# Five orders changed on ScalarE, VectorE and GpSimd in a transformer kernel of three-part products

## What the reference computes

```python
# first block
h = rms_norm(x, g) * (1 + sc1) + sh1
glu_in, qk_in, v, o_pre, if_pre, merge_pre = split(h @ w_in + b_in)
a = glu_in[..., :C] * sigmoid(glu_in[..., C:])
a = silu(layer_norm(causal_depthwise_conv(a, conv_dw_w, conv_dw_b)))   # 31 taps
y_conv = a @ w_conv_pw + b_conv_pw
hm = mlstm_chunkwise(q, k, v, i_pre, f_pre)                            # 4 heads
hm = (hm - mean(hm)) * rsqrt(var(hm) + EPS) * mlstm_norm_g             # per head
y = (g_conv * y_conv + g_mlstm * sigmoid(o_pre) * hm) @ w_out          # g_*: sigmoid(merge_pre)
# second block: mixer A with FFN, then mixer B with FFN
mem_n = rmsnorm(mem, g_mem)                                            # 256 memory rows
q, k, v, q_mem = split(rmsnorm(x, g_mix) @ b_w_in)                     # mixer B
q, k = apply_partial_rope(q), apply_partial_rope(k)
o = banded_window_attention(q, k, v)                                   # 16 heads, 4 key heads
x = x + concat(o, memory_cross_attention(q_mem, mem_n, w_mem_kv)) @ b_w_out
```

## Time and profile before

| | |
|---|---|
| Time, median of 3 runs | 2068.83 us |
| The profiled execution | 2069.17 us |
| Its span in the profile | 2067.4 us |
| TensorE busy | 2034.8 us (98 %) |
| VectorE busy | 1198.1 us (58 %) |
| ScalarE busy | 938.9 us (45 %) |
| GpSimd busy | 1018.3 us (49 %) |
| Granted clock of TensorE, mean | 0.998 |

### The profile page before, as it was taken

The page is one execution under the profiler, slowest core; times in us unless marked ns, Lnnn a source line. Parts: engine busy times, 40 slices in busy tenths (PEclk is TensorE's granted clock), DMA queues, the critical chain, the costliest instruction groups (busy, mean ns, idle before and its releaser), DMA issues.

```text
span 2067.4 us, 30134 instructions
## 1 busy us (share of the span) xinstructions
PE 2034.8 (98%) x11590; PEld 1743.2 (84%) x11590; DVE 1198.1 (58%) x2215; ACT 938.9 (45%) x1525; POOL 1018.3 (49%) x483
## 2 busy tenths in 40 slices
PE   9999999999999999999999999999999999999998
PEld 6888977788898989876877888989887588889997
DVE  4889788673642434476985463646423935545563
ACT  3345545363432334534366552434432956434343
POOL 3433432434675666443713575657344036665663
PEclk9999999999999999999999999999999999999999
DMA  9654322235233333332211433333433024333422
GB/s 370 241 183 143 103 62 62 87 103 175 70 102 102 107 98 103 96 110 66 80 24 52 127 102 97 98 113 93 147 92 74 2 85 114 103 102 102 122 73 92
DMA packets 282550, 220.91 MB, mean 107 GB/s; under 512 B 13520, under 2 KB 266576, under 8 KB 280112
## 3 DMA queue, kind: packets, MB, share of 16 engines
q1 hardware_dynamic: 271712, 195.75, 31.2%
q10 hardware_dynamic: 10704, 23.33, 3.7%
HBM read 213.56 MB, written 2.10 MB: 104 GB/s over the span
## 4 chain that ended last, share of the span: by engine, by line
PE 82%; DVE 8%; ACT 3%; POOL 3%; issue 2%; DMA 1%; ACTq 0%; SPq 0%; DVEq 0%; POOLq 0%
PE bank L1046 57%; PE bank L1123 11%; PE bank L1343 2%; PE bank L1534 2%; PE bank L1556 2%; DVE arena L3219 1%; PE bank L1491 1%; DVE small L3217 1%; PE bank L1543 1%; PE bank L1644 1%; POOL entry L3296 1%; PE bank L1391 1%; POOL w_split L3263 1%; DVE bank L2565 1%; PE bank L1402 1%
## 5 line engine op out<-in xcount | busy, mean ns | idle before, releaser
L1046 PE MATMUL bank<-h_hi,w_split 128*128 128x512 f32 x2832 | 865.3, 382 | 2.3 <-DVE arena L3087 1.1
L3263 POOL TENSOR_TENSOR w_split<-wslots,w_split 128x2048 fp32r<-128x2048 f32 (+3 forms) x119 | 470.1, 3951 | 648.2 <-ACT w_split L1798 636.6
L1046 PEld LDWEIGHTS bank<-h_hi,w_split 128*128 128x128 f32 x2832 | 534.7, 189 | 93.5 <-issue 16.2
L1046 PE MATMUL bank<-h_lo,w_split 128*128 128x512 f32 x1416 | 537.5, 380 | 0.0
L1798 ACT ACTIVATE w_split<-wslots 128x2048 fp32r<-128x2048 f32 (+2 forms) x114 | 194.1, 1702 | 367.9 <-PE bank L1046 314.9
L1046 PE MATMUL bank<-hid_hi,w_split 128*128 128x512 f32 x1056 | 316.5, 379 | 1.3 <-POOL w_split L3305 0.9
L1046 PEld LDWEIGHTS bank<-h_lo,w_split 128*128 128x128 f32 x1416 | 267.8, 189 | 38.7 <-issue 3.4
L1046 PEld LDWEIGHTS bank<-hid_hi,w_split 128*128 128x128 f32 x1056 | 199.6, 189 | 31.1 <-issue 1.6
L1046 PE MATMUL bank<-hid_lo,w_split 128*128 128x512 f32 x528 | 200.1, 379 | 0.0
L3296 POOL TENSOR_TENSOR entry<-entry_sum,entry 128x512 fp32r<-128x512 f32 x108 | 155.8, 1467 | 80.0 <-ACT entry L2121 80.0
L2565 DVE SCALAR_TENSOR_TENSOR bank<-arena,cols,bank 128x512 f32<-128x512 f32 x240 | 161.3, 750 | 5.4 <-ACT bank L1912 4.9
(11 more groups left out here) (376 smaller groups left out, 3142.5 us busy)
## 6 DMA issues: line engine op xcount, KB each, us to landing
wslots<-in_f_w_up SPq DMA_DIRECT2D x88, 512.0 KB, 5.0
wslots<-in_w_in SPq DMA_DIRECT2D x24, 1024.0 KB, 5.4
wslots<-in_w_ffn_up SPq DMA_DIRECT2D x44, 512.0 KB, 4.7
arena<-in_w_ada ACTq DMA_DIRECT2D x8, 2048.0 KB, 10.2
wslots<-in_a_w_in SPq DMA_DIRECT2D x10, 1024.0 KB, 5.3
arena<-in_w_ada_first SPq DMA_DIRECT2D x8, 1024.0 KB, 18.9
wslots<-in_f_w_down SPq DMA_DIRECT2D x8, 1024.0 KB, 5.1
wslots<-in_f_w_down SPq DMA_DIRECT2D x16, 512.0 KB, 4.0
```

Source lines behind the costliest of these rows:

```text
L1046: return nc.tensor.matmul(bank[:], w, woven(x), start=start, stop=stop)
L3263: last = nc.gpsimd.tensor_tensor(part[:, 1, cols_of], slot(p, 1, size)[:, 0, cols_of], part[:, 0, cols_of].bitcast(F32), ALU.subtract)
```

## The change

Five orders change; nothing is added to or left out of the computation.

- On VectorE, the last head's reciprocal goes ahead of the head's last four taps.
- On ScalarE, the split for the first conv_pw job (the one that `conv_gates(2)` began with) goes from behind the eighth upper of the convolution to behind the fifth.
- On ScalarE, the squares of the memory go ahead of the uppers of conv_pw job 0.
- On ScalarE, in the late stage of b_mix, the split that stood ahead of tile 6's upper goes behind that tile's square and copy.
- For mixer B's keys, ScalarE issues the four copies ahead of the value copies, both still behind the value product, and GpSimd rotates the keys ahead of the lower part of b_qmem.

```diff
@@ -2064,8 +2064,9 @@
                     last.then_inc(bank_free[one("merge_conv", 0)[0]], 1)
                 nc.scalar.activation(xT[:, c, :], conv(c), ACT.Square).then_inc(S["ln_square"], 1)
 
-            def conv_gates(j):
-                p = started("merge_conv", j)
+            def conv_gates(j, p=None):
+                if p is None:
+                    p = started("merge_conv", j)
                 for m in range(2):
                     last = nc.scalar.activation(halves(conv_gate[:, 2 * j + m, :]), plain(banks[2 * p + m][:]), ACT.Sigmoid, bias=col("b_merge", 2 * j + m))
                 last.then_inc(bank_free[p], 1)
@@ -2086,8 +2087,10 @@
             for c in range(1, DT):
                 activated(c)
                 conv_upper(c - 1)
+                if c == DT // 2 + 1:
+                    third = started("merge_conv", 2)
             conv_upper(DT - 1)
-            conv_gates(2)
+            conv_gates(2, third)
             conv_gates(3)
 
             def mixed_upper(j):
@@ -2096,10 +2099,10 @@
                     act.wait_ge(S["mixed_ready"], 2 * j + m + 1)
                     nc.scalar.activation(halves(mixed_split[0][:, 2 * j + m, :]), plain(banks[2 * p + m][:]), ACT.Copy).then_inc(S["mixed_hi_ready"], 1)
 
-            mixed_upper(0)
             act.wait_ge(S["mem_in"], 16)
             act.wait_ge(S["pool_tiles"], DT)
             nc.scalar.activation(mem_squares, memT.rearrange("p a b -> p (a b)"), ACT.Square).then_inc(S["mem_square"], 1)
+            mixed_upper(0)
             mixed_upper(1)
             act.wait_ge(S["row_sums"], 3)
             nc.scalar.activation(square[:, 0, 0:MEM // 4], banks[5][:, 0:MEM // 4], ACT.Sqrt, bias=con("eps", 1)).then_inc(S["rows_ready"], 1)
@@ -2252,14 +2255,17 @@
                     n = slot_after(FIRST[name] + j)
                     if j == 0:
                         nc.scalar.activation(small[:, 118 + LATE_NO[norm]:119 + LATE_NO[norm]], con("eps", 1), ACT.Sqrt)
+                    behind = norm == "b_mix" and j == DT - 2
                     if j + 2 in in_halves:
                         split_in_halves(n)
-                    elif j < DT - 1:
+                    elif j < DT - 1 and not behind:
                         split_job(n)
                     late_upper(act, norm, name, j)
                     if j == DT - 1:
                         split_job(n)
                     late_squares(act, norm, name, j)
+                    if behind:
+                        split_job(n)
 
             def memory_k(name, k):
                 out_of_job(name, 0, [(kv_of_mem[k][0][:, m, :], m, P, MEM) for m in range(2)])
@@ -2466,14 +2472,14 @@
             p, use = one("b_v", 0)
             act.wait_ge(S["late_cols_taken"], 1)
             act.wait_ge(product_done[p], use + 1)
+            act.wait_ge(S["rope_ready"], 28)
+            for head in (0, 64):
+                for half in (0, 64):
+                    act.dma_start(kw_heads[half:half + 64, head // 64:4:2, :], key_tiles[head:head + 64, :, :]).then_inc(S["dup_ready"], 16)
             for b in range(TB):
                 last = nc.scalar.activation(halves(v_groups[:, b, :]), plain(banks[2 * p + b // 2][:, (b % 2) * 2 * P:(b % 2 + 1) * 2 * P]), ACT.Copy,
                                             scale=small[:, 104 + b:105 + b])
             last.then_inc(bank_free[p], 1)
-            act.wait_ge(S["rope_ready"], 28)
-            for head in (0, 64):
-                for half in (0, 64):
-                    act.dma_start(kw_heads[half:half + 64, head // 64:4:2, :], key_tiles[head:head + 64, :, :]).then_inc(S["dup_ready"], 16)
             attend(2, "b_out")
             late_stage("b_out", "ffn2")
             if 2 in SEVEN:
@@ -2723,8 +2729,11 @@
                 head_taps(hd, 3)
                 square_of_root(hd)
                 gate_tile(4 * hd + 2)
+                if hd == HEADS - 1:
+                    inverse_of_root(hd)
                 head_taps(hd, 4)
-                inverse_of_root(hd)
+                if hd < HEADS - 1:
+                    inverse_of_root(hd)
                 gate_tile(4 * hd + 3)
             normalise(HEADS - 1)
 
@@ -3514,9 +3523,9 @@
             scaled_pair(2)
             lower_job("b_v", 0)
             scaled_pair(3)
-            lower_job("b_qmem", 0)
             emptied("b_k", 0)
             rope(KEYS, 2, P, 26)
+            lower_job("b_qmem", 0)
             lower_job("b_out", ahead("b_out"), 4)
             lower_job("b_out", 1 - ahead("b_out"), 4)
             split_weights("b_out", first=1)
```

## The result

The changed kernel takes 2072.72 us (median of 15 runs, 2070.51 to 2075.04) against 2069.29 of the kernel before (15 runs, 2067.84 to 2073.94): a ratio of 1.0015, 95 % interval 1.0009 to 1.0022. It is slower, by 1.9 to 4.6 us. That is within the 0.2 % which the prediction called no change, but the time lies 0.72 above its range (2066.0 to 2072.0). The profiled execution took 2075.01 (span 2073.2), near the upper end of the fifteen, so its 5.8 over the span before is more than the 3.1 of the ratio.

The account below looks back on a forecast made before the run. TensorE, busy 98 % of the span, was taken as the bound. +2.4 (third conv_pw job) + 1.2 (clock) - 0.7 (b_mix) - 1.1 (keys) = +1.8 gave 2071.0, or 2070.6 us on the median's footing; 8-in-10 range 2066.0 to 2072.0.

Parts of the forecast that it names:

- Reciprocal: Last head, VectorE: moved ahead of the taps, the job behind starts 0.35 us earlier, of a 1.20 wait; bounds 0 and 1.2.
- Split, hold and bank: Convolution to third conv_pw job: GpSimd's lower part holds VectorE's lowers, the bank comes late, the job starts 2.4 us later.
- The granted clock: Behind TensorE's 4.65 us idle before the third conv_pw job: a 1.2 GHz stretch costing 1.2 us, between 0 and 1.7.
- The rival with a lasting low clock: Third conv_pw job: 1.2 GHz for all 11.3 us of products costs 5.65 us, total 2075.0 us; chance 0.05.
- b_mix: Late b_mix: the upper follows residual tile 6 without waiting for the split, so TensorE's 0.7 us bank wait goes.
- The keys' copies: Mixer B's scores: copies issued 3.0 us earlier, sharing DMA engines with b_out's weights, gain 1.1 us; bounds 0.55 and 1.9.

Follow-up runs that it names:

- hold_pool: The changed kernel with GpSimd waiting for the eighth convolution lower before making the lower part of conv_pw job 0's weight; 2067.08 us, ratio 0.9989 to the kernel before.
- pieces: The changed kernel with GpSimd's lower part of conv_pw job 0's weight made in four pieces; 2070.22 us, ratio 1.0007 to the kernel before.
- its repeat: The changed kernel measured again, since the edit meant to delay b_out's second weight moved nothing; 2073.18 us, ratio 1.0021 to the kernel before.
- late_angle: The changed kernel with the fourth angle table computed behind VectorE's take of conv_pw job 0; 2066.02 us, ratio 0.9981 to the kernel before.
- keys_only: The kernel before with only the last keys' copies and rotation moved earlier; 2069.45 us, ratio 0.9997 to the kernel before.
- split_only: The kernel before with only the weight split moved behind the fifth upper; 2076.77 us, ratio 1.0038 to the kernel before.
- hold_bout2: The changed kernel with b_out's second weight issued only when the keys' copies have landed; 2069.34 us, ratio 0.9998 to the kernel before.
- fill: The changed kernel with 20 unread products added in TensorE's idle time before conv_pw job 2; 2070.01 us, ratio 1.0003 to the kernel before.
- best2: The changed kernel with the fourth angle table behind VectorE's take of conv_pw job 0 and b_out's second weight behind the keys' copies; 2061.93 us, ratio 0.9960.

## Why the prediction was wrong

Its direction and its mechanism were right: hold, late bank, new wait, low clock. Two terms of the sum were mis-sized, and both made the forecast too low. A further part of the miss is its footing: the forecast stood on the median of three runs, 2068.83, and fifteen runs put the kernel before at 2069.29, 0.46 higher.

- **Reciprocal.** Predicted 0.35 gained; the job behind it starts at 391.88, or 391.60 without the 0.28 of the start, in place of 392.07: 0.47. Right, by one profile; no run moves it alone.
- **Split, hold and bank.** Predicted: third conv_pw job 2.4 late, idle 4.65. Measured 2.2 to 2.5 and 4.84. Right, and shown by hold_pool and pieces to be GpSimd's instruction that holds VectorE's. By the Trainium skill's rule ("SBUF — State Buffer", "SBUF: two separate sides") the stage was to lose 2.4; the 5.24 for three lowers agrees with it.
- **The granted clock**, "so I price it at 1.2, between 0 and 1.7". This failed: 2.71 in the changed kernel, 2.07 in its repeat. I took the low stretch of the earlier trace rows, 3.3 us, as its length; here it lasted 6.8 us, of which 5.6 fell on products (4.3 in the repeat). One case is no bound for the length. The rival with a lasting low clock, at a chance of 0.05, came closer to the length: it was to decide from 7.1 us on.
- **b_mix.** Predicted 0.7 gained; the wait is gone. Right, by one profile as well.
- **The keys' copies**, "gain 1.1", bounds 0.55 to 1.9. This failed: 0.2 in the profile, none on the average. I added the two queues' engine time and let it start at once and end sharply; in the changed kernel the engines break off once at the start and thin out over some 1.5 us at the end, and the last copy lands after 7.4. The lower bound left out that sharing can eat all of the earlier issue. The DMA engines' busy share, 1582 to 1594, in tenths for each 0.3 us:

```profile
DMA  0000000049179999999999999999988522100000
```

With the measured terms, the 0.28 of the start left out, +2.2 + 2.7 - 0.7 - 0.2 = +4.0 in place of +1.8; with the repeat's 2.1 for the clock and nothing for the keys, +3.6. The two comparisons of this program give +3.1 (1.9 to 4.6) and +4.3 (2.3 to 6.2).

What stays open is what decides whether the clock falls behind a wait of 1.5 to 2.7. At the scores it fell in the changed kernel behind 1.68 and in late_angle behind 1.49, and stayed at 1.00 behind 1.88 and 2.67 (keys_only); at 1050 it fell behind 2.25 and stayed behind 2.27 in the changed kernel. So the length of the wait alone doesn't decide it.

## What to carry to other kernels

Before moving a weight's split earlier, look at what the engine that it wakes (GpSimd here) will then run beside: a 4.57 us instruction that lands on three short subtractions in SBUF delayed a queue, and with it a bank, 27 us later. Price a TensorE wait with the low clock behind it, by more than one case. And before issuing a transfer earlier, look at what else is on the DMA engines then: here copies issued 3 us earlier gained nothing beside a weight's transfer, and all of the wait once that transfer stood behind them.

## What the runs showed of the hardware

- VectorE's subtractions in SBUF and GpSimd's lower part of a weight held each other by the instruction: three lowers took 5.24 beside one GpSimd instruction of 4.57, 3.75 beside the same work in four (which then took GpSimd 6.37), and 2.0 with GpSimd idle.
- The five waits of TensorE from 3.46 to 6.80 us (the changed kernel, its repeat, pieces, split_only, hold_bout2) each had a stretch at 1.2 GHz behind them. It was 6.8 us long in each, began 2.3 to 4.1 us into the wait and ended with products running; the one of the earlier trace rows had lasted half of that. With products in the idle time (fill) the clock did not fall there.
- What part of the scatter of some 5 us between runs of one kernel is the clock's is not shown: best2's profile has it at 1.00 from the start to the last product, and its five runs lie within 2.2 us, but split_only's profile has three low stretches, and its five lie within 2.0.
